# A two-layer diffusion block: loading two gate/up pairs ahead of the fourth down load

## What is computed

```python
def swiglu(h, w_gate, w_up, w_down):
    return (jax.nn.silu(h @ w_gate) * (h @ w_up)) @ w_down

x = x + ga_a * (o @ w_out)
x = x + ga_f * swiglu(modulate(rms_norm(x, g_ffn), sh_f, sc_f), w_gate, w_up, w_down)
```

## Time and profile before

| what | value |
|---|---|
| median of 3 runs | 1813.56 us (1813.16 to 1814.61) |
| the profiled execution | 1813.76 us |
| its span in the trace | 1812.0 us |
| mean granted TensorE clock | 0.969 |
| feed-forward part, layer 0 / layer 1 | about 450 to 1060 us / 1425 to 1803 us |

### The profile page before, as it was taken

How to read it: one execution, slowest core, us unless ns; L and a number is a source line. 1 busy time by engine, 2 the same in 40 slices (tenths; PEclk the granted TensorE clock), 3 DMA queues, 4 the chain that set the end, 5 groups by cost and what they waited for, 6 DMA issues and landing times.

```text
span 1812.0 us, 28583 instructions
## 1 busy us (share of the span) xinstructions
PE 1659.4 (92%) x11013; PEld 1126.6 (62%) x11013; DVE 1056.5 (58%) x2071; ACT 756.6 (42%) x1362; POOL 787.3 (43%) x576
## 2 busy tenths in 40 slices
PE   7999989979899979997999989998979897996998
PEld 3688878867756646664666658887867443442444
DVE  4434499894388943858359753459985333223334
ACT  3222378863253331333313322237863453254252
POOL 2244355563523541434514234532435465465563
PEclk9999999999999989998999989999999998998999
DMA  9255443313225241344225223643003242152222
GB/s 318 41 137 138 122 125 90 88 48 88 64 82 163 82 127 37 117 151 140 82 83 176 89 48 83 147 121 77 2 16 102 71 128 74 56 150 58 70 82 82
DMA packets 317285, 179.17 MB, mean 99 GB/s; under 512 B 88526, under 2 KB 310494, under 8 KB 317150
## 3 DMA queue, kind: packets, MB, share of 16 engines
q1 hardware_dynamic: 284542, 143.63, 28.8%
q10 hardware_dynamic: 32608, 33.71, 5.8%
HBM read 158.97 MB, written 2.83 MB: 89 GB/s over the span
## 4 chain that ended last, share of the span: by engine, by line
PE 50%; DVE 9%; POOL 4%; issue 3%; ACT 3%; DMA 2%; SPq 1%; ACTq 0%; DVEq 0%; POOLq 0%
PE acc L940 45%; DMA pair_raw<-in_w_up 1%; POOL down_w L817 1%; POOL pair_w L801 1%; DVE stat L1888 1%; POOL pair_raw L798 1%; DVE prob_t L1902 1%; DVE mod_acc L2094 1%; DVE act L1726 1%; PE small L1228 1%; ACT squares_out L1528 1%; DVE scaled_ffn L1740 1%; POOL down_low L815 1%; PE side L1129 1%; ACT prob_t L1490 0%
## 5 line engine op out<-in xcount | busy, mean ns | idle before, releaser
L940 PE MATMUL acc<-act,pair_w 128*128 128x512 f16 x3168 | 581.2, 345 | 10.0 <-ACT act L1354 4.2
L940 PEld LDWEIGHTS acc<-act,pair_w 128*128 128x128 f16 x3168 | 308.1, 98 | 272.0 <-issue 9.9
L940 PE MATMUL acc<-act,split_w 128*128 128x512 f32 (+1 forms) x1920 | 378.0, 354 | 10.7 <-DVE act L2028 4.7
L940 PEld LDWEIGHTS acc<-act,split_w 128*128 128x128 f32 x1920 | 307.5, 189 | 63.4 <-DVE act L2028 6.9
L798 POOL TENSOR_SCALAR pair_raw<-pair_raw,weight_scale 128x1024 f32<-128x1024 f32 x88 | 111.2, 1263 | 355.1 <-ACT pair_w L1539 355.1
L940 PE MATMUL acc<-hidden,down_w 128*128 128x512 f16 (+1 forms) x1056 | 254.9, 351 | 5.0 <-POOL down_w L817 4.4
L2094 DVE SCALAR_TENSOR_TENSOR mod_acc<-mod_chunk,silu_c,mod_acc 128x256 f32<-128x256 f32 x280 | 196.6, 745 | 4.0
L801 POOL TENSOR_TENSOR pair_w<-pair_raw,pair_w 128x1024 f16<-128x1024 f32 x88 | 194.0, 2205 | 7.3
L690 POOL TENSOR_SCALAR split_w<-raw_w 128x1024 fp32r<-128x1024 f32 x72 | 78.1, 1085 | 260.9 <-PE acc L940 167.5
L2057 DVE SCALAR_TENSOR_TENSOR prod<-acc,prod_scale,silu_g 128x768 f32<-128x768 f32 (+1 forms) x44 | 38.9, 884 | 260.8 <-PE acc L940 198.9
L693 POOL TENSOR_TENSOR split_w<-raw_w,split_w 128x1024 fp32r<-128x1024 f32 x72 | 172.9, 2402 | 6.0
(11 more groups left out here) (221 smaller groups left out, 2335.8 us busy)
## 6 DMA issues: line engine op xcount, KB each, us to landing
mod_chunk<-in_w_mod ACTq DMA_DIRECT2D x28, 1024.0 KB, 5.0
pair_raw<-in_w_gate SPq DMA_DIRECT2D x44, 512.0 KB, 3.8
pair_raw<-in_w_up SPq DMA_DIRECT2D x44, 512.0 KB, 4.9
raw_w<-in_w_in SPq DMA_DIRECT2D x64, 256.0 KB, 3.8
raw_w<-in_w_mod SPq DMA_DIRECT2D x24, 512.0 KB, 4.1
raw_w<-in_w_down SPq DMA_DIRECT2D x20, 512.0 KB, 4.1
mod_start<-in_w_mod SPq DMA_DIRECT2D x8, 1024.0 KB, 10.7
ks<-q_split SPq DMA_DIRECT2D x64, 96.0 KB, 2.3
```

The costliest lines, as they stand in the source:

```text
L940: mm = pe.matmul(acc[slot][:, a:b], own, moving[:, part == 1, k, a:b], start=(k == 0 and part == 0), stop=(k == n - 1 and part == 1))
```

## The change

Three orders are changed, and no operation is added or removed.

- SyncE: the second pair of the next chunk (f0 + n + 1) is loaded right behind the first (f0 + n), ahead of down units 3 and 4.
- GpSimd: the two halves of that pair are split behind down unit 7, not behind units 3 and 4.
- ScalarE: down unit 0 is rounded behind silu of the last pair but one of the chunk, and down unit 1 behind silu of the last pair. Before, they stood at the end of the pair ahead of each. The third rounding stays.

```diff
--- before.py
+++ after.py
@@ -665,10 +665,9 @@
                                 load_down(ch, j)
                     if f0 + n < FT:
                         load_pair(f0 + n)
+                        load_pair(f0 + n + 1)
                     for j in range(3, KT):
                         load_down(ch, j)
-                        if j == 4 and f0 + n < FT:
-                            load_pair(f0 + n + 1)
             for t in range(4):
                 sp.wait_ge(y_act if t % 2 == 0 else y_dve, t // 2 + 1)
                 sp.dma_start(out[0, P * t:P * t + P, :], tokens[:, t, :]).then_inc(out_in, 16)
@@ -828,8 +827,9 @@
                         split_pair(f0 + n, 1)
                     for j in range(1, KT):
                         split_down(ch, j)
-                        if f0 + n < FT and j in (3, 4):
-                            split_pair(f0 + n + 1, j - 3)
+                    if f0 + n < FT:
+                        split_pair(f0 + n + 1, 0)
+                        split_pair(f0 + n + 1, 1)
 
 
         @block.tensor
@@ -1599,6 +1599,8 @@
                         sc.wait_ge(unit_done, u_pair(l, f, 0) + 1)
                         sc.activation(silu_g[:, 0:w], acc[0][:, 0:w], ACT.Silu, scale=weight_scale[:, 2, 2 * f:2 * f + 1]
                                       ).then_inc(silu_done, 1)
+                        if f >= f0 + n - 2:
+                            round_down(ch, f - (f0 + n - 2))
                         if l == 0 and f in LATE_AT:
                             late_chunk(LATE_AT.index(f), 1)
                         sc.wait_ge(prod_done, l * FT + f + 1)
@@ -1607,8 +1609,6 @@
                             round_down(ch, 2)
                         if f + 2 < FT:
                             round_pair(f + 2)
-                        if f0 + n - 3 <= f < f0 + n - 1:
-                            round_down(ch, f - (f0 + n - 3))
                     if ch < len(CHUNKS) - 1 or l == DEPTH - 1:
                         square_down(ch, 3)
                         for j in range(3, KT):
```

## The result

The changed kernel took **1768.75 us** (median of 4 runs, 1767.19 to 1770.69) against 1814.09 (median of 4, 1813.16 to 1814.79) for the kernel before: a ratio of 0.975, 95% interval 0.973 to 0.977. That is 45.3 us less, where 52.0 had been forecast; the time lies in the range. The profiled execution took 1770.69 us, its span is 1768.9, its mean granted clock 0.980. Sums from the two traces go by that one: 1812.0 - 1768.9 = 43.1 us.

A forecast was written before the change was run, and what follows sets the result against it. PE, busy 92%, was held by a 47.9 us wait at L973 for late squares behind a late pair load. Gains 15.5 + 16.1 + 10.1 + 7.8 + 5.7 = 55.2, less 3.2, gave 52.0, so 1761.6 us; range 1754 to 1776.

The forecast's parts named there:

- SP's part: Chunk boundaries: the next chunk's second pair load, issued near 1491 instead of 1507 in layer 1, is covered by PE's work.
- The sum of the fourth down unit as what is late next: At L981, four boundaries: PE's new wait, 1.4 to 3 us; gains counted there 15.5, 16.1, 10.1 and 7.8.
- 15.5 and 16.1: Layer 1, first and second boundary: us by which PE reaches the fourth down unit's sum earlier.
- a collision of DVE and POOL: Layer 0's modulation batches: moving POOL's work takes one collision away and adds one; 0.6 us cost for all four places.
- Clock behind the new waits: Behind the four new waits: clock drops at two of four places, 1.3 us each, 2.6 cost; ends 0 and 7.6.
- Rival 1: All four boundaries: the clock falls behind every new wait, gain 47.0 us, so 1766.6; chance 0.15.
- POOL's part: Layer 1, down units behind the sums: two 2.2 us waits for POOL and 1.3 of slow clock go, 5.7 us.
- ScalarE's part: Two down roundings moved behind silu: cost 0; ScalarE's 3.5 us wait for DVE no longer delays squares and silu.
- Batches in layer 0 that stretch (2): Layer 0: DVE's modulation batches lengthen, its two boundaries give nothing, gain 34.1 us, so 1779.5; chance 0.08.
- no new wait (3): Fourth down unit's sum: no new wait as ScalarE's pair rounding comes sooner, 8 us more, so 1753.6; chance 0.08.
- starving down units (4): Down units from the fifth on wait for loads, three raw buffers serving eight: 13.6 us slower, 1827.2; chance 0.04.
- nothing happens (5): SP is held by another wait ahead of the moved load, so nothing moves, 1813.6; chance 0.02.

The follow-up runs named there:

- early squares: Changed kernel with ScalarE's squares of the fourth down unit moved right behind silu and rounding of the last pair, in chunks with a next one: 1754.80 us, 0.967.
- the ninth experiment: Changed kernel with DVE's seven small scale instructions in a chunk's last pair moved behind hidden tile and third down scaling: 1773.01 us, 0.976.

## Why the prediction was right, and where it fell short

**SP's part: right.** The load was the bound, went where it was said, and is nearly the whole result: 42.5 us alone. That ScalarE's squares and silu come in time behind the early load was right at all four boundaries.

**The sum of the fourth down unit as what is late next: right in place, short in size.** The new waits were to be 3, 2.3, 1.4 and 1.3 us. They are 2.1 and 0.25 in layer 0 and 3.4 twice in layer 1. In layer 0's second boundary the wait moved ahead to silu (4.07) and the gain came out as forecast all the same, since both hang on DVE's batch.

**The step that failed**: "From the start of DVE's product to the end of that squaring it took ... 8.43 in layer 1", taken over as 8.5 for the new kernel with the words "none of which the change shortens". The change lengthens it, to 11.54. Two terms of the sum, 15.5 and 16.1, measured 12.3 and 12.9. The 8.43 had been measured while POOL stood idle behind the very load that was to be moved. The prediction did look for a collision of DVE and POOL, but only in layer 0's long batches, and there it took 0.6 us. That the holds are the cause is more than a match of rows: with POOL held back, two of the three instructions are at their old durations, and the kernel is 6.4 us faster, of which 4.6 are PE's waits in layer 1 and part of the rest is clock; with the squares out of that chain the two boundaries give 15.9 and 16.4, close to the 15.5 and 16.1 of the sum.

The rule cited there, of the Trainium skill, "SBUF — State Buffer", section "SBUF: two separate sides" (the shared port pair is locked for a whole instruction), fits these rows: every held instruction ends within 0.03 us of an end of POOL's. By that rule the price of a meeting is set by the length of POOL's instruction and not by the size of DVE's, and the traces agree with 1.86 us on 128 x 1 elements and 2.17 on 128 x 8. They also show what the prediction did not weigh: which of DVE's instructions are held differs, and the neighbours L1975 and L1977 passed at 0.15 and 0.21.

**Clock behind the new waits: the term was 2.6, it measured 4.6.** The forecast was half clock at two of four places, and it was two of four new waits at the sum. But the gaps were longer, and the second cost 3.0 us by itself, where 1.3 had been taken. Rival 1 (the clock falls behind every new wait, 1766.6) came nearest to the time, partly by luck: the first sum of layer 0 kept its clock, and the greater part of the shortfall, 6.4 us, is not clock.

**POOL's part: the sum right, the account not additive.** 5.7 was forecast and 6.4 measured at the marks of the full change. But the same microseconds came for the most part with the load alone: the parts alone give 42.5, 7.6 and, for the first rounding, nothing: 50.1 together against 45.3.

**ScalarE's part: "cost taken: 0" holds, "that is why both sit in the sums above" does not.** The 1.2 us that PE lost one pair earlier were booked as gained. They are gained in time, but what follows is bounded by the chain of DVE and POOL, and taking the part out again changes the time by less than a measurement tells (2.4 us by the marks).

**The other rivals.** Batches in layer 0 that stretch (2), no new wait (3), starving down units (4), nothing happens (5): none came. The ring of three raw buffers held: none of the units five to eight made PE wait at the four boundaries.

**Open**: the profiled executions differ from each other by up to 5.7 us ahead of the first boundary, and by up to 4.4 in the attention part between the layers, where no kernel was changed, and I have not explained it; it is why places are compared between marks. Nor is it settled what decides the clock behind a short gap (below).

## To carry to other kernels

When a long wait is removed, a chain measured behind it was measured on a quiet machine: for each engine that shares a resource with the chain, ask where it will stand at that moment once the wait is gone, and lay its instructions beside the chain's. Small DVE instructions between two steps of a critical chain are exposed to POOL's long ones, and it is cheaper to take the dependent work out of the chain (14 us here, early squares) than to reorder the small instructions (nothing). Parts of a change that are worth nothing behind a bound can be worth much once it is gone: POOL's and ScalarE's parts bring 3.5 us to the load alone and 13.7 with the early squares, so a part is best judged again after each bound that falls. The best version found is the full change with the early squares, 1754.8 us against 1768.75 for the change and 1815 for the kernel before.

## What I had not expected of the hardware

- A DVE instruction on 128 x 1 elements that takes 0.15 us took 1.86 beside POOL's 128 x 1024 subtraction of 2.12, and a TENSOR_SCALAR on 128 x 2 took up to 2.12, each to within 0.03 us of POOL's end. RECIPROCAL, the int32 one and the TENSOR_SCALAR on 128 x 1 (L1977) in the same stretch were not held. The 128 x 1024 scaling takes 1.28 us alone and took 1.54 to 3.18 beside POOL. POOL is held in turn: its subtraction takes 2.12 alone and 3.08 in the fence of the ninth experiment.
- The clock behind a short gap is not a matter of the gap's length alone. I counted the gaps in the pairs and down units of all fourteen traces. Of seventeen gaps of 2.0 to 2.25 us, the mean clock of the next 4 us was 0.57 to 0.67 behind ten and 1.00 behind seven; of twelve of 3.2 to 3.4 us, it was 0.50 to 0.63 behind eleven and 1.00 behind one; behind those of 0.95 to 1.8 us it stayed at 1.00. Two more gaps stand at the same place in all fourteen, and there the next 4 us were always slow: 2.48 us among layer 0's pairs near 500 us (0.50 to 0.64), and only 1.69 us ahead of layer 1's first pair (0.50 to 0.65). At both, PE had stood still twice shortly before (2.1 and 0.6 us, 1.5 and 0.6 us). In the kernel with SP's and POOL's edits it fell behind 2.09 us in layer 0, where the changed kernel kept it behind the same 2.09, and it was kept behind the second of two gaps of 3.21 in layer 1. These are its stretches behind the first sum of layer 0 and the second of layer 1:

```profile
652.00:656.00 4.00, 4.00 (x16) 1.96 (x14) 1.42 (x3) 2.77 (x5) 2.41 (x2) 0.57 0.36 107
1633.80:1637.80 4.00, 4.00 (x20) 1.85 (x21) 2.52 (x6) 2.89 (x4) 1.66 (x2) 1.00 0.46 131
```

By the marks a fall cost 1.3 to 1.7 us at most places and 3.0 at the second sum of layer 1 in the changed kernel. An estimate does well to carry one for every new gap of 2 us or more as its bound, and to take it as likely above 3; the 1.69 shows that 2 us is no safe limit. What decides between two equal gaps no run here shows.
